# Rounds of a top selection moved from an attention stage into the projection before it, and table products left out of its differential steps

## The reference, cut to what matters

```python
proj = h @ w_in[l]
(fq, fk, fv, ff, dq, dk, dv, sq, sk, sv, iq, ik, iw) = jnp.split(proj, split_points, axis=-1)
...
o_fox = fox_attention(fq, fk, fv, cum_logf)      # 6 heads of 64, forget gates
o_diff = diff_attention(dq, dk, dv, lam)         # 4 heads, two maps of width 32 each
o_dsa = dsa_attention(sq, sk, sv, iq, ik, iw, topk)   # 6 heads of 64, one key head
```

```python
score = jnp.einsum('bqh,bhqk->bqk', wib, jax.nn.relu(s_idx))
score = jnp.where(mask[None], score, -jnp.inf)
_, sel = lax.top_k(score, topk)
```

## Time and profile before

| | |
|---|---|
| Median of three runs | 2389.19 us (2388.99 to 2390.48) |
| The profiled execution | 2388.17 us, span on the core 2386.5 us |
| Mean granted TensorE clock | 0.994 of full speed |
| Busy, share of the span | TensorE 96%, VectorE 54%, ScalarE 39%, GpSimd 11% |
| Chain that ended last | TensorE 82% of the span, VectorE 10%, ScalarE 3% |
| First layer | last products of the input projection to 155.7 us, attention from 156.6 to about 303 |
| Second layer | last products of the input projection to 849.8 us, attention from 850.6 |

### The profile page before, as it was taken

One profiled execution on the slowest core, in us unless ns is written; L12 is line 12 of the kernel. 1 busy time (PEld: TensorE's weight loads), 2 busy tenths in 40 slices (PEclk: granted clock), 3 DMA queues, 4 the chain that ended last, 5 costly groups with the idle time before them and its releaser, 6 DMA issues.

```text
span 2386.5 us, 32760 instructions
## 1 busy us (share of the span) xinstructions
PE 2291.7 (96%) x13381; PEld 1868.6 (78%) x13381; DVE 1278.8 (54%) x1864; ACT 928.3 (39%) x1555; POOL 272.1 (11%) x175
## 2 busy tenths in 40 slices
PE   6999899999999998999999999999999999999998
PEld 6776688888888775688888888896676888887777
DVE  4678448863225577359843154215555363126774
ACT  3446642222214356642222232324544242115664
POOL 2001212121001012122121000000000000001210
PEclk9999999999999999999999999999999999999999
DMA  5210015632223210035523321321000124223311
GB/s 154 85 66 2 1 55 193 195 123 88 106 90 98 75 36 1 20 134 165 194 88 103 110 63 55 101 79 47 15 14 14 56 71 139 71 71 56 61 30 53
DMA packets 144614, 189.51 MB, mean 79 GB/s; under 512 B 41141, under 2 KB 94402, under 8 KB 144450
## 3 DMA queue, kind: packets, MB, share of 16 engines
q1 hardware_dynamic: 108816, 168.26, 21.5%
q10 hardware_dynamic: 35586, 19.01, 3.5%
q0 software_dynamic: 64, 0.16, 0.0%
HBM read 179.94 MB, written 7.47 MB: 79 GB/s over the span
## 4 chain that ended last, share of the span: by engine, by line
PE 82%; DVE 10%; issue 3%; ACT 3%; POOL 1%; ACTq 0%; DMA 0%; DVEq 0%; POOLq 0%
PE ps L488 63%; PE ps L1729 3%; PE ps L2271 2%; DVE ps L1926 2%; PE ps L1768 2%; PE ps L1733 2%; DVE probs_t L1956 1%; PE ps L2300 1%; PE ps L1782 1%; PE ps L2288 1%; DVE score L2158 1%; PE ps L495 1%; DVE top L2155 1%; PE ps L684 1%; DVE sink_part L1916 1%
## 5 line engine op out<-in xcount | busy, mean ns | idle before, releaser
L464 DVE TENSOR_TENSOR w_low<-w_raw,w_high 128x2048 fp32r<-128x2048 f32 (+4 forms) x140 | 304.6, 2176 | 509.7 <-ACT w_high L459 509.5
L459 ACT ACTIVATE w_high<-w_raw 128x2048 fp32r<-128x2048 f32 (+4 forms) x140 | 253.0, 1807 | 621.4 <-PE ps L488 607.9
L488 PE MATMUL ps<-h_hi,w_high 128*128 128x512 f32 x976 | 371.5, 381 | 1.6 <-DVE h_lo L2655 0.9
L488 PE MATMUL ps<-h_lo,w_high 128*128 128x512 f32 x976 | 369.1, 378 | 0.0
L488 PE MATMUL ps<-h_hi,w_low 128*128 128x512 f32 x976 | 368.9, 378 | 0.0
L488 PE MATMUL ps<-w_high,h_hi 128*128 128x512 f32 (+3 forms) x736 | 276.9, 376 | 6.3 <-DVE w_low L464 5.6
L488 PE MATMUL ps<-w_low,h_hi 128*128 128x512 f32 (+3 forms) x736 | 274.3, 373 | 0.0
L488 PE MATMUL ps<-w_high,h_lo 128*128 128x512 f32 (+3 forms) x736 | 274.0, 372 | 0.0
L488 PEld LDWEIGHTS ps<-h_hi,w_high 128*128 128x128 f32 x976 | 183.7, 188 | 37.2 <-issue 1.4
L488 PEld LDWEIGHTS ps<-h_hi,w_low 128*128 128x128 f32 x976 | 183.5, 188 | 34.8
L488 PEld LDWEIGHTS ps<-h_lo,w_high 128*128 128x128 f32 x976 | 183.7, 188 | 34.1 <-issue 0.5
(11 more groups left out here) (325 smaller groups left out, 3779.0 us busy)
## 6 DMA issues: line engine op xcount, KB each, us to landing
w_raw<-in_w_gate_up SPq DMA_DIRECT2D x44, 1024.0 KB, 5.2
ada_w<-in_ada_w SPq DMA_DIRECT2D x24, 1024.0 KB, 5.1
w_raw<-in_w_down SPq DMA_DIRECT2D x20, 1024.0 KB, 4.8
w_raw<-in_w_in SPq DMA_DIRECT2D x16, 1024.0 KB, 5.0
w_raw<-in_c_in_w SPq DMA_DIRECT2D x16, 1024.0 KB, 5.5
w_raw<-in_w_out SPq DMA_DIRECT2D x8, 1024.0 KB, 4.8
w_raw<-in_ab_in_w SPq DMA_DIRECT2D x8, 1024.0 KB, 5.1
bias<-bias_scratch ACTq DMA_DIRECT2D x32, 224.0 KB, 5.0
```

Source lines behind the costliest of these rows:

```text
L459: e.activation(w_high[j % 2][:, 0:size], w_raw[j % 2][:, 0:size], ACT.Copy).then_inc(sig.w_high_done, 1)
L464: e.tensor_tensor(w_low[j % 2][:, 0:size], w_raw[j % 2][:, 0:size], w_high[j % 2][:, 0:size].bitcast(F32), ALU.subtract).then_inc(sig.w_lo ...
L488: mm = e.matmul(dst, lhs, rhs, start=start and a == 0, stop=stop and a == 2)
```

## The change

Three edits. In the projection, `RowsOut` gets a `vector` of its own that runs rounds of the selection on tile 1: five before the copy of the last tile of group 3, two before tile 1 of group 4 and four before its tile 3. In the attention stage the 37 other rounds are spread over the same steps. The table products ahead of the differential scores are left out; the other table products of the stage stay.

```diff
@@ class InProduct
             rounds = [(t, c) for t in range(1, NT) for c in range(IH // 2)]
+            EARLY_ROUNDS = {(3, 3): 5, (4, 1): 2, (4, 3): 4}
@@ class RowsOut
+            def vector(self, e, B, L, st, i, ch):
+                for n, m, t0, nt in st.order():
+                    if n % 2:
+                        if (i, n) in st.EARLY_ROUNDS:
+                            e.wait_ge(sig.idx_used, B["idx_used"] + 4)
+                            for _ in range(st.EARLY_ROUNDS[i, n]):
+                                top_round(e, ch, 1)
+                        self.need(e, B, st, n)
+                        self.put(e, self.dst(i, m, t0), ps[:, st.bank(i, n), 0:st.columns(i)], 1, m)
+
@@ CausalPairs.tensor
                         e.wait_ge(sig.turned_second, B["turned_second"] + s - self.SETS + 1)
-                    if x.kind == "diff":
-                        keep_warm(e, self.bank(s, 0), 2)
                     q, k = q_turned[x.group % 2], kd_turned if x.kind == "dsa" else k_turned[x.group % 2]
@@ CausalPairs.vector
-                done, rounds = 0, 3 * ROUNDS
+                early, rounds = sum(InProduct.EARLY_ROUNDS.values()), 3 * ROUNDS
+                done = early
                 for s in range(-2, self.N):
...
-                    share = min(rounds, rounds * (s + 3) // self.ROUND_STEPS)
+                    share = min(rounds, early + (rounds - early) * (s + 3) // self.ROUND_STEPS)
                     while done < share:
                         top_round(e, ch, 1 + done // ROUNDS)
                         done += 1
```

## The result

The changed kernel takes 2369.28 us (median of 4 runs, 2368.14 to 2371.03); the kernel before, run beside it, 2389.09 (4 runs, 2387.62 to 2390.48). The ratio is 0.9917, with a 95% interval of 0.9905 to 0.9928: 19.8 us saved. 2366.0 was forecast, with a range of 2360 to 2377. The profiled execution took 2371.03 (span 2369.4) against 2388.17 (span 2386.5), so its span is shorter by 17.1.

What follows compares the result with a forecast made beforehand. TensorE bounds the kernel (96% busy); in differential stretches VectorE's rounds limit from about the middle to the mask. Gains of 10.2 + 9.8 + 3.2 = 23.2 us give 2364.97 from the profiled 2388.17, 2366.0 as median, range 2360 to 2377.

Steps and rivals of the forecast that it cites:

- The projection, 0: Input projection: eleven added rounds, 13.1 us of VectorE per layer, hide in its idle time and cost 0.
- TensorE's units, 46.3: Four differential units: without table products TensorE needs 10.74, 11.77, 11.40 and 12.43, a floor of 46.3 us against 58.57.
- VectorE to the mask, 48.4: Differential stretch: VectorE's rounds and maxima release the mask at 48.0, plus 0.4 for gaps; gains 10.2 and 9.8 us.
- The clock behind the mask wait, 3.2: First sparse work: mask wait shrinks to 1 or 1.5 us, clock stays at 2.4 GHz, 2.1 + 1.1 = 3.2 us back.
- The rule that spoke against it: Differential stretch: activity releases the throttled clock, so gap-filling products help pay for it; the sum could lose 3.2 and more.
- the slower rival: Differential units: without table products the clock falls, stretch about 73, 14.5 longer per layer, 2418 us; chance 0.07.
- TensorE's floor: Differential stretch: TensorE's own work sets 46.9, giving 2363; with the forget units' end, the range's lower end of 2360.
- A fall only behind a wait near 3 us: Whole trace: rows show the clock falling only after a wait near 3 us, so the sum keeps its 3.2.
- Stages couple: Differential units: maxima late behind double rounds delay ScalarE's copies, stretch 50.5, 2373.4 us; chance 0.20 with clock still lost.
- VectorE stops being the limit: Differential stretch: gaps between VectorE's instructions fill better, TensorE's floor of 46.9 holds, 2363 us; chance 0.09.

Runs made afterwards that it cites:

- e6: Changed kernel with all 16 rounds of tile 1 in the projection (7, 3 and 6 at the three places), 32 left for attention: 2380.12 us, 0.996 of before.
- e1: Changed kernel with the table products ahead of the differential scores put back, the eleven rounds staying in the projection: 2379.52 us, 0.996 of before.
- e9: Changed kernel with one round moved from step 24 to step 23, still 18 rounds in the differential units: 2372.37 us, 0.9927 of before.
- e12: e3 with its last two rounds set together on step 24, none at step 23, 13 in the differential units as before: 2371.48 us, one run.
- e11: The changed kernel itself measured once more, nothing altered: 2368.39 us, 0.9915 of before.
- e3: Changed kernel with most of attention's 37 rounds made in the forget units, 13 instead of 18 left for the differential steps: 2366.55 us, 0.9905 of before.
- e8: The kernel of e4 once more, for its trace (changed kernel, eight table products ahead of the mask wait): 2368.75 us, one run.
- e2: Kernel before without the table products of the differential steps, all 48 rounds staying in attention: 2389.67 us, 1.0007 of before.
- e4: Changed kernel with eight table products issued ahead of the wait for the keep mask: 2368.97 us, 0.9916 of before.
- e7: Changed kernel with all 16 early rounds in one place, ahead of the copy of group 3's last tile: 2393.17 us, 1.0017 of before.
- e5: e3 with four table products ahead of the wait for the keep mask: 2366.76 us, 0.9907 of before.
- e10: Kernel before with one round moved from step 24 to step 23: 2390.03 us, one run.

## Why the prediction was right, and where it was off

*The projection, 0.* Right. The eleven rounds are hidden in both layers; the two copies that were to move by 0.5 and 0.1 moved by 0.3 and not at all. Five more rounds are no longer hidden (e6).

*TensorE's units, 46.3.* A little low, because a pair of products was priced at its full 0.55: units 3 and 4 lost 1.99 and 1.80, not 2.20 each, which agrees with the 6.0 that e1 shows for the 16 pairs. The first three are 10.95, 12.17 and 11.87 where 10.74, 11.77 and 11.40 were taken; the fourth is 14.02 less its wait of 1.68, 12.34, where 12.43 was taken. The sum is 47.3, so TensorE is 1.7 under the stretch and not 2.1.

*VectorE to the mask, 48.4.* This term carried most of the sum and was short by 0.6. (The prediction counts the rounds from the maxima of step 12 on, 21 of them; the 18, 16 and 13 of the experiments are those behind the maxima of step 14 on.) The units' first maxima start at 208.88, 221.70 and 233.19 in the changed kernel and the masks end at 244.78 + 0.89 = 245.67, so the three pieces are 12.82, 11.49 and 12.48; forecast were 12.8, 11.05 and 12.2, behind a start at 11.9 that was 12.1. The masks end 48.91 into the stretch instead of 48.0, so the 0.4 for gaps should have been 1.0: there is a hole of 0.23 for TensorE's scores and one of 0.29 that belongs to no wait. The gain of the two stretches is 9.6 + 9.2 = 18.8 and not 20.0. The reason was right as far as it went, by e9, but it named one limit where e12 shows two.

*The clock behind the mask wait, 3.2.* This step failed: it gave nothing in this trace and 0.8 in e11's. Two things were wrong in it. The price was set by comparing 7.34 and 6.35 with 5.92 less a GpSimd wait of 0.66, 5.26; at full clock that wait is there in this piece too (0.65 at 251.68 above), so a fall costs 1.4 and 0.4, not 2.1 and 1.1. And behind the 1.88 of layer 2 the clock fell as before (6.32 against 6.35). In layer 1 it did not, but then it fell behind the sum over the pair, 27 us later, and took 1.5 back. From the first sparse scores to the output projection it takes 50.33 against 50.27 before in layer 1 and 49.25 against 49.28 in layer 2; in e11, 49.29 and 49.45. In a layer without any fall it takes 48.8 (e3 in layer 1, e8 in layer 2), so 1.5 and 0.5, 2.0 in all, was the most that the clock had to give back.

So 18.8 of the 23.2 are found in the traces. Of the profiled pair 1.0 is lost at the start and 0.6 behind the second layer's attention, which leaves 17.1; the medians differ by 19.8. e11's trace, which began like the one before, is 20.2 shorter than before: 18.8 in the stretches, 0.8 from the clock behind the masks, 0.2 at the start and 0.4 behind the second layer's attention. The last two lie where the change edits nothing.

*The rule that spoke against it, and the slower rival.* In the changed kernel the granted clock is 1.00 through both stretches, so the rival's place shows no fall. But it is no empty rival: e2 has just that fall, to 0.50 from 236.7 to 257.2 in layer 1 and for 10 us in layer 2, and with it the removal of the products is worth nothing. What differs is the 1.3 to 1.6 us waits, which are 0.7 at most in the changed kernel until the mask; that they bring the fall is argued from these rows, and no run tests it by itself. The prediction took 0.66 for the longest wait inside a unit; the kernel before has one of 1.20, for GpSimd's spread at 244.03, with its table products in place and the clock at 1.00 behind it. What the Trainium skill says (TensorE: Matmul & The Clock Gate, The HAM clock gate), that activity is what releases the throttle, agrees with e2 in half: the fall came among waits, but the clock then stayed at 0.50 for 20 us in which the rows count TensorE as busy nearly throughout. In these runs the removal of table products paid only where no longer wait took their place. The chance of 0.07 was for the whole change and I find no fault with it. Two of the smaller sums are loose and bear on nothing else: 69 us of products and the 6.4 of waits make a stretch of 75 and not 73, and TensorE's floor less 1 us per layer for the forget units is 2361 and not 2360.

*A fall only behind a wait near 3 us.* The prediction held this against the rule. It was read from two places; the same trace has a fall at 1683.35 in the second block, behind a wait of 1.44, and one at 1594.60 behind no wait at all (last section).

*Stages couple; VectorE stops being the limit.* The first did not happen in the changed kernel: its 50.5 was not reached. The second needs another spread of the rounds; e3 went half the way to its 46.9.

## What to carry to other kernels

When two engines have nearly equal loads up to one join, measure each part of a change beside the whole: here the parts gave 8.9 and -1.3, and together 19.8. At such a join count two chains of the feeding engine, its total of work and the tail behind the last input that it needs; keep filler work out of the tail. And don't book a clock that comes back before its whole consequence is read: take the wait that was hidden under the slow products into the price, and look where it falls next.

## What was not expected of the hardware

In this attention stage the clock falls in one of two places, and in a few stages in both. The granted clock of the changed kernel in windows around the two candidates of layer 1, the piece behind the mask and that behind the products of two columns that sum over a pair:

```profile
245.77:253.77 8.00, 7.04 (x58) 4.97 (x58) 1.49 (x5) 5.36 (x14) 1.88 (x2) 1.00 0.01 2
272.84:281.84 9.00, 9.00 (x68) 6.92 (x68) 1.62 (x3) 6.78 (x15) 1.30 (x3) 0.81 0.00 0
```

the same two places of layer 1 in the second trace of the same kernel, e11:

```profile
244.59:252.59 8.00, 8.00 (x55) 5.68 (x56) 1.46 (x4) 5.03 (x14) 1.87 (x2) 0.79 0.01 2
272.14:281.14 9.00, 9.00 (x80) 6.79 (x78) 1.81 (x3) 7.63 (x19) 1.32 (x3) 1.00 0.01 2
```

With waits for the mask of 1.68 and 1.69, one kernel fell in either place. Of the 26 attention stages in thirteen traces (all but e4's) ten fell at the mask alone, nine behind the pair sum alone, four in both (layer 2 of e7 and e9, both layers of e6), two in neither, and in one, e2's first, the clock was just coming up. So of 14 stages that fell at the mask four fell behind the pair sum too, and of 11 that did not, nine. All 14 had waited 1.68 or more for the mask. Where the wait for the mask was 1.33 or less, or filled (e1, e3, e5, e8), none of the eight stages fell at the mask, and six of them fell at the pair sum. What went before the second of the two falls is not idle time, by the rows of the changed kernel:

```profile
272.84 1.95 PE L2325 MATMUL ps<-con,proj 128*128 128x2 f32 x16
...
275.69 1.41 PE L2297 MATMUL ps<-con,probs 128*128 128x128 f32 x8
277.04 1.55 PE L2309 MATMUL ps<-probs_t,proj 128*64 128x128 f32 x12
```

Sixteen products of two columns hold TensorE for 1.95 us by its busy time, and 2.9 us after their start the eight transposes behind take 1.41 where they take 1.03 to 1.09 at a granted clock of 1.00. The second block has a like place. These rows of the kernel before stand between products of 384 columns, without a wait:

```profile
1592.18 2.90 PE L1262 MATMUL ps<-ones,lat_sum 128*128 128x1 f32 x24
1594.94 0.67 PE L488 MATMUL ps<-w_high,lat_hi 128*128 128x384 f32 x1
1595.40 0.52 PE L488 MATMUL ps<-w_high,lat_lo 128*128 128x384 f32 x1
```

The granted clock is 1.00 up to 1594.60 and 0.50 from there to 1598.02, and products that took 0.33 take 0.52. In seven of the thirteen traces (before, changed, e2, e6, e7, e10, e12) a fall begins 2.1 to 2.5 us after the start of these 24 products of one column. So products of one or two columns stand ahead of the fall in both places, and the rows count TensorE as busy in both. Whether they are its cause is left open: no run put other work there, and in six traces nothing falls behind the 24.

From the first sparse scores to the output projection a fall at the mask alone costs 0.4 to 2.1 us, one behind the pair sum alone 1.5 to 1.6 and both 2.6 to 3.6, against the 48.8 without a fall. A fall may come in either layer, so gains under some 2 us are better read from a stretch than from a median.
